# A two-block transformer kernel on one core: the FFN product turned in 32x32 blocks by VectorE and moved through a DRAM buffer

## The reference, cut to what matters

```python
def rms_norm(x, g):
    y = x32 * lax.rsqrt(jnp.mean(x32 * x32, axis=-1, keepdims=True) + EPS)
    return (y * g.astype(jnp.float32)).astype(x.dtype)

def swiglu(h, w_gate, w_up, w_down):
    return (jax.nn.silu(h @ w_gate) * (h @ w_up)) @ w_down
...
x = x + 0.5 * swiglu(rms_norm(x, g[0]), ffn_w_gate[i, 0], ffn_w_up[i, 0], ffn_w_down[i, 0])
```

## Time and profile before

| | |
|---|---|
| time, median of 3 runs | 1400.75 us (1399.75 to 1401.27) |
| the profiled execution, its own time | 1400.78 us |
| its span in the profile | 1399.0 us |
| PE busy | 1343.9 us, 96% |
| DVE busy | 794.5 us, 57% |
| ACT busy | 644.3 us, 46% |
| DMA, bytes moved | 233.29 MB, mean 167 GB/s |

### The profile page before, as it was taken

The page is one execution under the profiler, slowest core; times in us unless marked ns, Lnnn a source line. Parts: engine busy times, 40 slices in busy tenths (PEclk is TensorE's granted clock), DMA queues, the critical chain, the costliest instruction groups (busy, mean ns, idle before and its releaser), DMA issues.

```text
span 1399.0 us, 17530 instructions
## 1 busy us (share of the span) xinstructions
PE 1343.9 (96%) x6634; PEld 1113.6 (80%) x6634; DVE 794.5 (57%) x861; ACT 644.3 (46%) x729; POOL 76.3 (5%) x180
## 2 busy tenths in 40 slices
PE   6999999999999998999999999999998998999996
PEld 5888889877888886788888767888886986788885
DVE  4545458646554456555446865554456787554453
ACT  5443357325434445543444844434445555434442
POOL 2000003100000001000000210000001200000000
PEclk9999999999999999999999999999999999999999
DMA  8555554414655554355554323655553452555550
GB/s 264 185 198 188 180 196 151 151 61 153 223 188 180 189 199 152 128 196 187 180 188 140 124 91 123 223 188 180 190 200 122 138 181 65 181 190 185 191 194 30
DMA packets 159116, 233.29 MB, mean 167 GB/s; under 512 B 7528, under 2 KB 126462, under 8 KB 159070
## 3 DMA queue, kind: packets, MB, share of 16 engines
q1 hardware_dynamic: 156420, 229.19, 49.0%
q10 hardware_dynamic: 2170, 2.68, 0.6%
q0 software_dynamic: 480, 0.80, 0.2%
HBM read 231.58 MB, written 1.05 MB: 166 GB/s over the span
## 4 chain that ended last, share of the span: by engine, by line
PE 89%; DVE 6%; ACT 3%; issue 1%; DMA 1%; POOL 0%; SPq 0%; POOLq 0%; ACTq 0%; DVEq 0%
PE ps L231 26%; PE ps L233 26%; PE ps L232 26%; DVE wl L203 2%; PE ps L473 2%; ACT wh L198 2%; PE ps L315 1%; PE ps L247 1%; PE ps L840 1%; PE ps L248 1%; PE ps L249 1%; DVE x_rows L415 1%; DMA raw<-in_ffn_w_up 1%; PE ps L1351 1%; ACT hth L335 0%
## 5 line engine op out<-in xcount | busy, mean ns | idle before, releaser
L231 PE MATMUL ps<-wl,hth 128*128 128x512 f32 (+2 forms) x1280 | 506.9, 396 | 13.1 <-DVE htl L348 6.7
L233 PE MATMUL ps<-wh,htl 128*128 128x512 f32 (+2 forms) x1280 | 497.2, 388 | 0.0
L232 PE MATMUL ps<-wh,hth 128*128 128x512 f32 (+2 forms) x1280 | 496.8, 388 | 0.0
L611 DVE TENSOR_TENSOR wl<-raw,wh 128x2048 fp32r<-128x2048 f32 x120 | 275.0, 2292 | 204.8 <-ACT wh L563 204.8
L231 PEld LDWEIGHTS ps<-wl,hth 128*128 128x128 f32 x1280 | 242.2, 189 | 64.0 <-issue 10.6
L563 ACT ACTIVATE wh<-raw 128x2048 fp32r<-128x2048 f32 x120 | 229.6, 1914 | 123.7 <-PE ps L233 123.7
L203 DVE TENSOR_TENSOR wl<-raw,wh 128x2048 fp32r<-128x2048 f32 (+3 forms) x100 | 221.2, 2220 | 108.3 <-ACT wh L198 108.2
L233 PEld LDWEIGHTS ps<-wh,htl 128*128 128x128 f32 x1280 | 242.0, 189 | 49.7
L232 PEld LDWEIGHTS ps<-wh,hth 128*128 128x128 f32 x1280 | 242.4, 189 | 45.2
L198 ACT ACTIVATE wh<-raw 128x2048 fp32r<-128x2048 f32 (+3 forms) x100 | 184.6, 1854 | 70.1 <-PE ps L233 49.6
L231 PE MATMUL ps<-wl,prod_h 128*128 128x512 f32 x400 | 156.1, 390 | 0.0
(11 more groups left out here) (351 smaller groups left out, 958.5 us busy)
## 6 DMA issues: line engine op xcount, KB each, us to landing
raw<-in_ffn_w_gate SPq DMA_DIRECT2D x88, 512.0 KB, 4.0
raw<-in_ffn_w_up SPq DMA_DIRECT2D x88, 512.0 KB, 4.9
raw<-in_ffn_w_down SPq DMA_DIRECT2D x88, 512.0 KB, 3.8
raw<-in_w_gate_up SPq DMA_DIRECT2D x44, 512.0 KB, 4.7
raw<-in_even_w_in SPq DMA_DIRECT2D x24, 512.0 KB, 4.5
raw<-in_w_down SPq DMA_DIRECT2D x22, 512.0 KB, 3.8
raw<-in_ple_w_gate SPq DMA_DIRECT2D x16, 512.0 KB, 3.7
raw<-in_w_in SPq DMA_DIRECT2D x16, 512.0 KB, 4.4
```

The costliest lines, as they stand in the source:

```text
L231: nc.tensor.matmul(o, xh, b, start=first, stop=False)
L232: nc.tensor.matmul(o, xh, a, start=False, stop=False)
L233: return nc.tensor.matmul(o, xl, a, start=False, stop=last)
L611: nc.vector.tensor_tensor(wl[:, r, :], raw[:, r, :], wh[:, r, :].bitcast(f32), ALU.subtract)\
```

## The change

The product is no longer turned by PE, except for product 10 of each FFN. `turn_blocks` on VectorE transposes it within blocks of 32x32, with one instruction, from `prod` into the first half of `xn[:, 0, :]`. A 32x32 block transpose leaves each block in its group of 32 partitions; the groups are exchanged by two DMAs that ScalarE starts: `move` writes the 128 x 512 floats (256 KB, rows of 2 KB) to a DRAM buffer `bounce`, and `fetch` reads them back into `xn[:, 1, 0:512]` (512 runs of 512 bytes). `high` and `low` then read that copy and not the bank. The layout of `prod_h` and `prod_l` changes from [column tile, row] to the earlier trace rows, and `down` takes its pieces accordingly. `fetch`, `high` and `low` of a product stand in the next round of the loop: in ScalarE's loop `fetch(c - 1)` is the first thing and `high(c - 1)` comes behind split 1, `move(c)` is the last.

```diff
--- before.py
+++ after.py
@@ -105,6 +105,10 @@
         minus_half = sb("minus_half", [P, 16])
         p_high = sb("p_high", [P, 2, T], f32r)
         p_low = sb("p_low", [P, 2, T], f32r)
+        prod_blocks = xn[:, 0, 0:512]
+        bounce = nc.dram_tensor("bounce", [P, 512], f32).ap()
+        prod_moved = xn[:, 1, 0:512]
+        moved_tiles = prod_moved.rearrange("p (q g t) -> p g q t", q=4, g=4)
         vnorm = sb("vnorm", [P, 512])
         onorm = sb("onorm", [P, 128])
         qk_norm = sb("qk_norm", [P, 2, 64])
@@ -146,6 +150,9 @@
         silu_ready = sem("silu_ready")
         prod_ready = sem("prod_ready")
         prod_turned = sem("prod_turned")
+        blocks_ready = sem("blocks_ready")
+        blocks_out = sem("blocks_out")
+        blocks_moved = sem("blocks_moved")
         prod_high = sem("prod_high")
         prod_low = sem("prod_low")
         gain_loaded = sem("gain_loaded")
@@ -443,6 +450,9 @@
                         sp.dma_start(dst, src).then_inc(raw_loaded[(n + 2 + j) % RING], 16)
             load_slot(sp, n + FFN_SLOTS - 1, down(n + FFN_SLOTS - 1, 2 * (NCH - 1)))
 
+        def prod_tiles(v):
+            return v[:, :, :].rearrange("p t (k q m) -> p (t k) q m", k=2, q=4)
+
         def ffn_pe(pe, n, s, f):
 
             def gate_up(place, k, b=0):
@@ -452,12 +462,16 @@
 
             def down(place, first, last, halfway=None):
                 h, l = (last_h, last_l) if last else (prod_h, prod_l)
+
+                def columns(v, kk, tt):
+                    return v[:, kk, tt * P:(tt + 1) * P] if last else v[:, tt, kk * P:(kk + 1) * P]
+
                 pieces = [(kk, tt, half) for kk in range(2) for tt in range(TT) for half in range(2)]
                 if last:
                     pieces.sort(key=lambda v: v[2])
                 for i, (kk, tt, half) in enumerate(pieces):
                     at = kk * D + half * 512
-                    m = product(bank(4 + 2 * tt + half), h[:, kk, tt * P:(tt + 1) * P], l[:, kk, tt * P:(tt + 1) * P],
+                    m = product(bank(4 + 2 * tt + half), columns(h, kk, tt), columns(l, kk, tt),
                                 wh[:, place % RING, at:at + 512], wl[:, place % RING, at:at + 512],
                                 first and kk == 0, last and kk == 1)
                     if last and i == 3:
@@ -485,7 +499,6 @@
                 down(n + 4, first, False)
 
                 pe.wait_ge(prod_ready, c + (f * NCH + 1))
-                turn_product()
 
 
             turn_x(pe, s, 0, FFN_BANKS[0])
@@ -508,15 +521,10 @@
                 take_slot(pe, n + 2 + half)
                 for kk in range(4):
                     gate_up(n + 2 + half, 4 * half + kk, 2)
-                if half == 0:
-
-                    pe.wait_ge(prod_ready, f * NCH + 1)
-                    turn_product(0)
             pe.wait_ge(prod_low, f * NCH + 1)
             take_slot(pe, n + 4)
             down(n + 4, True, False)
             pe.wait_ge(prod_ready, f * NCH + 2)
-            turn_product()
             with pe.Fori(2, NCH - 1) as c:
                 chunk(c, False)
 
@@ -549,10 +557,24 @@
                 for tt in range(TT):
                     nc.scalar.activation(silu_g[:, tt, :], ps[:, b + tt, 0:HC], ACT.Silu, scale=rstd[:, tt:tt + 1]).then_inc(silu_ready, 1)
 
-            def high(c, b=2, to=prod_h):
-
-                act.wait_ge(prod_turned, c + (f * NCH + 1))
-                nc.scalar.activation(to[:, :, :], bank(b).rearrange("p (k t) -> p k t", k=2), ACT.Copy)\
+            def move(c):
+
+                act.wait_ge(blocks_ready, c + (f * (NCH - 1) + 1))
+                act.dma_start(bounce, prod_blocks).then_inc(blocks_out, 16)
+
+            def fetch(c):
+                act.wait_ge(blocks_out, c * 16 + (f * (NCH - 1) + 1) * 16)
+                act.dma_start(prod_moved.rearrange("p (q c) -> p q c", q=4),
+                              bounce.rearrange("(q n) (r c) -> (n r) q c", q=4, r=4)).then_inc(blocks_moved, 16)
+
+            def high(c):
+
+                act.wait_ge(blocks_moved, c * 16 + (f * (NCH - 1) + 1) * 16)
+                nc.scalar.activation(prod_tiles(prod_h), moved_tiles, ACT.Copy).then_inc(prod_high, 1)
+
+            def high_last():
+                act.wait_ge(prod_turned, f + 1)
+                nc.scalar.activation(last_h[:, :, :], bank(2).rearrange("p (k t) -> p k t", k=2), ACT.Copy)\
                   .then_inc(prod_high, 1)
 
             def split(c, j):
@@ -568,23 +590,30 @@
             act_ahead.through(act, n + 3)
             rms(act, s)
             silu(n + 2)
+            move(0)
             act_ahead.through(act, n + 4)
-            high(0, 0)
+            fetch(0)
+            high(0)
             act_ahead.through(act, n + 5)
             silu(n + 4, 2)
             act_ahead.through(act, n + 6)
-            high(1)
+            move(1)
             with act.Fori(2, NCH - 1) as c:
+                fetch(c - 1)
                 split(c, 1)
+                high(c - 1)
                 split(c, 2)
                 silu(c * 3 + (n + 1))
                 split(c, 3)
-                high(c)
+                move(c)
             act_ahead.n += 3 * (NCH - 3)
+            fetch(NCH - 2)
+            act_ahead.through(act, n + FFN_SLOTS - 2)
+            high(NCH - 2)
             act_ahead.through(act, n + FFN_SLOTS - 1)
             silu(n + 3 * (NCH - 1) + 1)
             act_ahead.through(act, n + FFN_SLOTS)
-            high(NCH - 1, to=last_h)
+            high_last()
             if s + 1 in ple_of:
                 turn_act(act, s + 1, 0, 2, dst=p_high, banks=(3,))
             act_ahead.before(act, n + FFN_SLOTS - 1)
@@ -598,11 +627,22 @@
                                                        in1=silu_g[:, tt, :], op0=ALU.mult, op1=ALU.mult)
                 m.then_inc(prod_ready, 1)
 
-            def low(c, b=2, to=prod_l, high=prod_h):
+            def turn_blocks(c):
+
+                dve.wait_ge(prod_ready, c + (f * NCH + 1))
+                nc.vector.transpose(prod_blocks.rearrange("p (r g t) -> p g r t", r=4, g=4),
+                                    prod[:, :, :].rearrange("p t (k n r) -> p (t k) r n", k=2, r=4)).then_inc(blocks_ready, 1)
+
+            def low(c):
 
                 dve.wait_ge(prod_high, c + (f * NCH + 1))
-                nc.vector.tensor_tensor(to[:, :, :], bank(b).rearrange("p (k t) -> p k t", k=2),
-                                        high[:, :, :].bitcast(f32), ALU.subtract).then_inc(prod_low, 1)
+                nc.vector.tensor_tensor(prod_tiles(prod_l), moved_tiles, prod_tiles(prod_h).bitcast(f32),
+                                        ALU.subtract).then_inc(prod_low, 1)
+
+            def low_last():
+                dve.wait_ge(prod_high, (f + 1) * NCH)
+                nc.vector.tensor_tensor(last_l[:, :, :], bank(2).rearrange("p (k t) -> p k t", k=2),
+                                        last_h[:, :, :].bitcast(f32), ALU.subtract).then_inc(prod_low, 1)
 
             def split(c, j):
                 r = (n + j) % RING
@@ -614,23 +654,27 @@
             norm_dve(dve, s, FFN_GAIN[f], FFN_BANKS)
             dve_ahead.through(dve, n + 3)
             multiply(0)
+            turn_blocks(0)
             dve_ahead.through(dve, n + 4)
-            low(0, 0)
+            low(0)
             dve_ahead.through(dve, n + 5)
             multiply(1, 2)
+            turn_blocks(1)
             dve_ahead.through(dve, n + 6)
-            low(1)
             with dve.Fori(2, NCH - 1) as c:
                 split(c, 1)
+                low(c - 1)
                 split(c, 2)
                 multiply(c)
+                turn_blocks(c)
                 split(c, 3)
-                low(c)
             dve_ahead.n += 3 * (NCH - 3)
+            dve_ahead.through(dve, n + FFN_SLOTS - 2)
+            low(NCH - 2)
             dve_ahead.through(dve, n + FFN_SLOTS - 1)
             multiply(NCH - 1)
             dve_ahead.through(dve, n + FFN_SLOTS)
-            low(NCH - 1, to=last_l, high=last_h)
+            low_last()
             if s + 1 in ple_of:
                 turn_dve(dve, s + 1, 0, 2, dst=p_low, dst_h=p_high, banks=(3,))
             add_result(dve, s, 0.5 if f < 4 else 1.0)

```

## The result

The changed kernel takes 1405.09 us (median of 7 runs, 1401.68 to 1406.86) against 1400.82 us for the kernel before (7 runs, 1399.75 to 1401.74). The ratio is 1.0028, with a 95% interval of 1.0016 to 1.0040: 0.3% slower, where 1.5% faster was forecast.

The account below looks back on a forecast made before the run. The prediction took the kernel to be bound by TensorE's instruction stream. From 1400.8 us it took off 23.0 for the removed turns and added 1.5 for late first products, giving 1379.3 us, range 1376 to 1392.

Parts of the forecast that it names:

- The turn: On PE, four transposes of a product: 0.46 us each by the chunk period, 50 removed, 23.0 us gained.
- The cover in the chunks: In the steady loop, the bounced product is ready 5 us before PE wants it, so the detour costs nothing.
- W: ScalarE's write of the product to `bounce`, from issue to landing, taken as 2.7 us.
- R: The read of the product back from `bounce`, from issue to landing, taken as 3.2 us.
- The first product of each FFN: At `down(0)`, where cover is shorter: 0.15 us late in the third FFN, counted as 1.5 us in all, from 0 to 15.
- T: VectorE's block transpose of one product, taken as 0.7 us, with 2.3 kept for the range.
- Rival A: First products much later, by upper-end transfers or a write held up by weight loads: 15 us late, 1385 to 1393; chance 0.13.
- Rival B: DRAM round trip outlasts the cover in every chunk: slower, 1525 us at 7.3 us per transfer, anything above 1403; chance 0.07.
- C: The 23 us vanish because PE waits for weights or its loop jump comes to light: 1394 to 1402; chance 0.05.
- The sign given for this case: PE idle before `down`'s first product on `prod_h`, released by ScalarE or VectorE only five times, would mean a late first product.

## Why the prediction was wrong

**The turn** (0.46 us, 23.0 in all): right. The round fell by 0.48 us, and without the exchange the kernel gained 23 us. Reading it from the period and not from the durations (54 us) held.

**The cover in the chunks** ("I cost all of it at nothing"): right in its result, PE never waited in a round of the loop in the profile, and 45 trips were free. The terms were too small: W and R are 4.2 and 5.1 us in the median, not 2.7 and 3.2, so the cover was nearer to 3 than to 5 us (in the round shown above `low` ended at 652.6 and PE wanted it at 656.0), and the experiment with held loads used it up twice.

**The first product of each FFN** ("I count 0.3 × 5 = 1.5 us, from 0 to 15"): this is the step that failed. It was 19.6 us of waiting, outside even the upper bound. T was 1.09 us, not 0.7, between L604's row and the estimate of 1.24 us from the Trainium skill ("VectorE: DVE Perf Modes", "The three transpose paths"), and the chip was near the latter. W and R were 5.7 and 4.6 us there, not 2.7 and 3.2. In the third FFN the three terms add 0.4, 3.0 and 1.4 us to the 0.15 of the forecast, 4.9 us in all, where PE waited 4.73: the write is the larger part. The bounds came from rows of transfers with no weight load beside them: the store of `out` is the last thing the kernel does, and beside the loads of `in_p` SyncE's queue moves nothing. I named the load of 577.16 as being in the air, and did not charge it. The trace of the kernel before could have priced it. SyncE's queue from 577 to 580:

```profile
q1 hardware_dynamic: 1083, 1.08, 106.4%
```

A load of 1 MB keeps all the engines at work for some 3 us, and the kernel's own order puts one ahead of each of the two trips. With them out of the way the step's numbers come true: write 2.4, read 2.8, no wait for product 0, 1379.7 us, against a forecast of 1379.3.

**The clock** was not in the sum at all. Rival A had the mechanism (late first product, write behind the loads) with a ceiling of 1393 and a chance of 0.13. To its waits of 15 us I should have added what follows them. The measured 1405 is A, with 19.6 us of waits and 10.3 us in the rounds behind them, less some 4 us of clock in other stages, whose tie to the change no run shows. The exact working of the clock (which wait brings it down for how long, and why it falls in other stages in some kernels) stays open.

**Rival B** (the trip outlasts the cover in every chunk) and **C** (nothing comes back) are refuted by the round of 16.32 us. The sentence that a result above 1403 would be B was wrong: it was A. The sign given for this case was right: the idle row ahead of `down` came exactly five times.

## What to carry to other kernels

When work is moved off the bound engine onto a longer path, the steady loop tells the gain and the first pass tells the loss: look for the iteration whose consumer follows soonest, and treat that one separately. Here leaving 5 of 50 turns where they were kept 21 of the 23 us. Price a new DMA by its place among the transfers already in flight, not by a row from a quiet stretch, and order the loads that nobody is waiting for behind it. To a wait of TensorE add the clock it may cost.

## What the runs showed of the hardware

- TensorE's granted clock fell to 0.50 behind waits of 4.06 to 4.97 us in the middle of a kernel that otherwise kept it busy, and the next round then took 17.8 to 19.3 us instead of 16.32; behind the wait of 1.28 us the round took 16.49. Shorter waits went both ways: behind 1.99 and 2.04 us the round took 18.09 and 18.05, behind 2.18 us 16.49. Filled with useless products, the same stretch stayed at 1.00.
- The same 256 KB write landed after 2.4 us without and after 5.7 to 5.9 us with a weight load issued some 2 us ahead of it, though it was in another engine's queue.
- A block transpose of 128x512 float32 with a source stride of four elements took 1.08 to 1.13 us on VectorE.
- Run to run the changed kernel spread over 5.2 us, the kernel before over 2.0.
